# A two-block transformer kernel on one core: the on-chip buffers are laid out in another order, and one operand is packed more tightly

## The reference, cut to what matters

```
h = x
h = layer_norm(a*h + sparse_attention(h));  h = layer_norm(a*h + mlp(h))      # layer A, 16 heads, top-128 keys
h = layer_norm(a*h + gated_linear(h));      h = layer_norm(a*h + mlp(h))      # layer B, 4 heads, chunks of 64
# second block
p    = modulate(rms_norm(h)) @ w_in
mix  = concat[attention(8 heads), bidirectional_mlstm(4 heads)] @ w_out
h    = h + g1 * mix
h    = h + g2 * (silu(u @ w_gate) * (u @ w_up)) @ w_down,   u = modulate(rms_norm(h))
out  = rms_norm(h) * g
```

## Time and profile before

| | |
|---|---|
| time, three runs | 1869.84, 1871.6, 1872.71 us, median 1871.6 us |
| the profiled execution | 1871.6 us, its span from first to last instruction 1869.8 us |
| granted clock of TensorE, mean | 0.997 |
| busy | PE 98%, DVE 61%, ACT 40%, POOL 6% |
| moved by DMA | 189.34 MB, mean 101 GB/s |

### The profile page before, as it was taken

How to read it: one execution, slowest core, us unless ns; L and a number is a source line. 1 busy time by engine, 2 the same in 40 slices (tenths; PEclk the granted TensorE clock), 3 DMA queues, 4 the chain that set the end, 5 groups by cost and what they waited for, 6 DMA issues and landing times.

```text
span 1869.8 us, 22776 instructions
## 1 busy us (share of the span) xinstructions
PE 1825.8 (98%) x9140; PEld 1490.0 (80%) x9140; DVE 1132.9 (61%) x1953; ACT 744.2 (40%) x1177; POOL 117.3 (6%) x117
## 2 busy tenths in 40 slices
PE   9999999999999999999999999999998999999998
PEld 7775788888888888878888888778656898888886
DVE  4987676555557687577654455786766543333338
ACT  4548343222333543645322233365655452222222
POOL 0341000000000063000000000000011000000000
PEclk9999999999999999999999999999999999999999
DMA  6220415434443121141533333222102313223221
GB/s 211 68 74 30 169 46 203 135 135 144 160 146 115 46 86 51 50 154 46 180 113 131 117 113 120 85 90 93 46 24 78 114 45 114 90 91 112 90 91 45
DMA packets 120185, 189.34 MB, mean 101 GB/s; under 512 B 7800, under 2 KB 72536, under 8 KB 117008
## 3 DMA queue, kind: packets, MB, share of 16 engines
q1 hardware_dynamic: 118688, 183.08, 29.5%
q0 software_dynamic: 1392, 4.82, 0.9%
HBM read 185.72 MB, written 2.16 MB: 100 GB/s over the span
## 4 chain that ended last, share of the span: by engine, by line
PE 83%; DVE 10%; ACT 5%; issue 2%; DMA 0%; DVEq 0%; ACTq 0%
PE bank L652 10%; PE bank L654 10%; PE bank L653 10%; PE bank L841 7%; PE bank L843 7%; PE bank L842 7%; PE bank L626 3%; PE bank L628 3%; PE bank L627 3%; PE bank L901 2%; PE bank L876 2%; DVE gb L2306 2%; PE bank L674 2%; PE bank L885 2%; PE bank L676 2%
## 5 line engine op out<-in xcount | busy, mean ns | idle before, releaser
L1945 DVE TENSOR_TENSOR wl<-raw,wh 128x2048 fp32r<-128x2048 f32 (+1 forms) x137 | 308.4, 2256 | 203.1 <-ACT wh L1296 202.7
L1296 ACT ACTIVATE wh<-raw 128x2048 fp32r<-128x2048 f32 (+1 forms) x142 | 265.3, 1882 | 225.5 <-PE bank L843 89.0
L652 PE MATMUL bank<-xh,wh 128*128 128x512 f32 (+1 forms) x872 | 340.1, 390 | 1.1 <-DVE wl L1945 1.1
L654 PE MATMUL bank<-xl,wh 128*128 128x512 f32 (+1 forms) x872 | 339.3, 389 | 0.0
L653 PE MATMUL bank<-xh,wl 128*128 128x512 f32 (+1 forms) x872 | 339.3, 389 | 0.0
L841 PE MATMUL bank<-wh,uh 128*128 128x512 f32 x592 | 230.4, 389 | 0.5 <-DVE wl L1945 0.5
L842 PE MATMUL bank<-wl,uh 128*128 128x512 f32 x592 | 230.3, 389 | 0.0
L843 PE MATMUL bank<-wh,ul 128*128 128x512 f32 x592 | 230.3, 389 | 0.0
L652 PEld LDWEIGHTS bank<-xh,wh 128*128 128x128 f32 (+1 forms) x872 | 163.3, 187 | 37.5 <-DVE wl L1945 1.9
L654 PEld LDWEIGHTS bank<-xl,wh 128*128 128x128 f32 (+1 forms) x872 | 163.3, 187 | 34.5
L653 PEld LDWEIGHTS bank<-xh,wl 128*128 128x128 f32 (+1 forms) x872 | 163.3, 187 | 34.1
(11 more groups left out here) (362 smaller groups left out, 2945.0 us busy)
## 6 DMA issues: line engine op xcount, KB each, us to landing
raw<-in_mlp_w_up SPq DMA_DIRECT2D x32, 1024.0 KB, 6.1
raw<-in_mlp_w_down SPq DMA_DIRECT2D x32, 1024.0 KB, 5.0
raw<-in_w_ada SPq DMA_DIRECT2D x24, 1024.0 KB, 5.0
raw<-in_b_w_in SPq DMA_DIRECT2D x12, 1024.0 KB, 5.2
raw<-in_w_gate SPq DMA_DIRECT2D x11, 1024.0 KB, 5.2
raw<-in_w_up SPq DMA_DIRECT2D x11, 1024.0 KB, 5.1
raw<-in_w_in SPq DMA_DIRECT2D x10, 1024.0 KB, 5.0
raw<-in_w_down SPq DMA_DIRECT2D x10, 1024.0 KB, 4.9
```

Source lines behind the costliest of these rows:

```text
L652: pe.matmul(o, H[:, k, c], xh[:, k, :], start=k == 0, stop=False)
L654: step = pe.matmul(o, H[:, k, c], xl[:, k, :], start=False, stop=k == 7)
L1296: act.activation(slots[slot_of[i]][0][:, 0:n], raw[:, i % NRAW, 0:n], ACT.Copy).then_inc(*s_high.up(i))
L1945: dve.tensor_tensor(L[:, 0:n], raw[:, i % NRAW, 0:n], H[:, 0:n].bitcast(F), ALU.subtract).then_inc(*s_low.up(i))
```

## The change

The declarations are put in another order, `margin` and `end` go, `A` grows from 13312 to 13344 numbers a partition, the rows of `vx` shrink from 144 to 130 numbers (so that the matmul streams whole rows, still 130), and what lay behind `vx` in `A` moves down by 224 numbers. `Mr` gets the 512 numbers that this leaves at the end of `A`, in place of a range within the first 2048 numbers.

```diff
         h = sb("h", [P, T, D])
+        with nc.sbuf_tensor("xf", [P, 8192], F) as xf:
+            pass
+        xh = sb("xh", [P, 8, SEQ], R)
+        xl = sb("xl", [P, 8, SEQ], R)
         raw = sb("raw", [P, NRAW, CH])
+        wh = sb("wh", [P, NHL, CH], R)
+        wl = sb("wl", [P, NHL, CH], R)
...
+        C = sb("C", [P, C_END])
         LM = sb("LM", [P, 8 * P], U8)
-        rot = sb("rot", [P, 2, T, 16])
...
+        gb = sb("gb", [P, 2048])
         small = sb("small", [P, 648])
...
-        sb("margin", [P, 56])
-        gb = sb("gb", [P, 2048])
...
-        with nc.sbuf_tensor("A", [P, 13312], F) as A:
+        with nc.sbuf_tensor("A", [P, 13344], F) as A:
             pass
...
-        sb("end", [P, 1024])
...
-        inv_b = [A[:, 12032:12544], A[:, 12544:13056]]
+        inv_b = [A[:, 11808:12320], A[:, 12320:12832]]
...
-        vx = A[:, 9728:12032].rearrange("p (t h n) -> p t h n", t=T, h=4)
+        vx = A[:, 9728:11808].rearrange("p (t h n) -> p t h n", t=T, h=4)
...
-        kd2 = A[:, 12032:13056].rearrange("p (t n) -> p t n", t=T)
-        Mr = [A[32 * d:32 * d + 4, 1536:2048] for d in range(2)]
+        kd2 = A[:, 11808:12832].rearrange("p (t n) -> p t n", t=T)
+        Mr = [A[32 * d:32 * d + 4, 12832:13344] for d in range(2)]
...
-                            step = pe.matmul(bank[b][:, o:o + 130], STm[m % 2][:, q, t * P:(t + 1) * P], vx[:, q, hh, 0:130],
+                            step = pe.matmul(bank[b][:, o:o + 130], STm[m % 2][:, q, t * P:(t + 1) * P], vx[:, q, hh, :],
```

More of the change, by code:

```diff
@@ L320, in program @@
         h = sb("h", [P, T, D])
-        raw = sb("raw", [P, NRAW, CH])
-        LM = sb("LM", [P, 8 * P], U8)
-        rot = sb("rot", [P, 2, T, 16])
[L324 to L341, removed]
-        sb("margin", [P, 56])
-        gb = sb("gb", [P, 2048])
         with nc.sbuf_tensor("xf", [P, 8192], F) as xf:
@@ L348, in program @@
         xl = sb("xl", [P, 8, SEQ], R)
+        raw = sb("raw", [P, NRAW, CH])
         wh = sb("wh", [P, NHL, CH], R)
@@ L358, in program @@
         ul = sb("ul", [P, 2, 4, SEQ], R)
-        with nc.sbuf_tensor("A", [P, 13312], F) as A:
+        C = sb("C", [P, C_END])
+        LM = sb("LM", [P, 8 * P], U8)
+        gb = sb("gb", [P, 2048])
+        small = sb("small", [P, 648])
+        stats = sb("stats", [P, T, 2, 6])
+        mv = sb("mv", [P, T, 2])
+        rsv = sb("rsv", [P, 64])
+        rsy = sb("rsy", [P, 64])
+        rsa = sb("rsa", [P, 64])
+        rsh = sb("rsh", [P, 64])
+        posi = sb("posi", [P, T], I32)
+        rot = sb("rot", [P, 2, T, 16])
+        iw = sb("iw", [P, T, 8])
+        m8 = sb("m8", [P, 8])
+        att = sb("att", [P, 3, 16, T])
+        ssq = sb("ssq", [P, T, 4])
+        ebl = sb("ebl", [P, 4, 4])
+        s32 = sb("s32", [P, 16])
+        root = sb("root", [P, 16])
+        epsilon = sb("epsilon", [P, 2])
+        q_rms = sb("q_rms", [P, 32])
+        gg = sb("gg", [P, T, 16])
+        g2_ = sb("g2_", [P, T, 16])
+        acol = sb("acol", [P, 2, T, 4])
+        ecol = sb("ecol", [P, 2, T, 4])
+        den = sb("den", [P, 2, 2, 2])
+        with nc.sbuf_tensor("A", [P, 13344], F) as A:
             pass
```

## The result

| | before | after |
|---|---|---|
| median of 5 runs | 1871.6 us (1869.84 to 1874.81) | 1883.14 us (1882.68 to 1883.57) |
| ratio, 95% interval | | 1.0062, 1.005 to 1.0074 |
| profiled execution, its span | 1871.6, 1869.8 us | 1881.6, 1879.8 us |
| mean granted clock | 0.997 | 0.998 |

The forecast was 1871.6 us with a range of 1868 to 1877. The measured time lies beyond it on the slow side.

What follows compares the result with a forecast made beforehand. PE was taken to bound the kernel, as a sum over some 9140 matmuls in fixed order. Every part of the change came to 0 us, so the 1869.8 us span plus 1.8 around it gave 1871.6 us, range 1868 to 1877.

Steps and rivals of the forecast that it cites:

- What bounds the kernel: Whole kernel: PE, 98% busy, runs some 9140 matmuls in fixed order; 512 columns take 0.2257 us, 12.4 ns not columns.
- The instruction streams: All five engines: same operations, shapes and waits in the same order, so nothing may start earlier; 0 us.
- `vx`: Rows at 520 bytes, streamed by 160 matmuls of L1203: starts 8 past a multiple of 16 cost 0 us.
- DVE and ACT: Buffers 32 past a multiple of 64: convolution starts at nearly any multiple of 4 cost at most 8 ns; 0 us.
- POOL: L2885 and L2903 at the new starts: taken as 0 us, with ends of -0.9 and +0.9.
- DMA: Transfers to `gb`, `A` and `C` at new offsets: 0 to 0.4 us, taken as 0; 0.04 us for each spread.
- Weight loads: PE loads from buffers 32 past a multiple of 64: hidden beside the matmul before unless 38 ns longer; 0 us.
- Moving operands of PE: 1,552 matmuls streaming from `A`, `gb`, slots 2 and 3: taken as 0; upper end a second 12.4 ns each, 19.2 us.
- rival A: Those 1,552 PE matmuls slow down when streaming from 32 past 64: 1881.2 us at half, 1890.8 at whole; chance 0.11.
- Buffers now 128 past a multiple of 256, and other distances between buffers: `xh` to `pl` and `C`: starts at any multiple of 64, and where another buffer lies, cost PE nothing; 0 us.
- Rival B: mLSTM stage: PE's pause and clock drop near 1412 us go or grow; if gone, 1866.3 us, chance 0.05.
- C: Rope and gate jobs start earlier as `Mr` shares no queries' bytes; held impossible, 1871.6 us; chance 0.74 with the forecast.
- D: DMA pays for the starts: 0.4 us on the chain, 1 us in the mLSTM stage, 1873.0 us; within a shared 0.08.

Runs made afterwards that it cites:

- e4c_A_same_mod256: The kernel after with `A` moved on by 96 bytes: 1871.47 us against 1871.72 for the kernel before, ratio 1.0002.
- e3_before_all_plus32: The kernel before with everything from `xh` to `A` moved on by 32 bytes: 1872.58 us against 1873.20, ratio 0.9999.
- e2_before_A_plus32: The kernel before with only `A` moved on by 32 bytes: 1882.78 us, ratio 1.0054.
- m2c_differences: TensorE alone, no kernel: 48 split matmuls per operand pair, buffers 2048 bytes apart, differences in 16-byte steps; 226.7 ns a matmul at difference 0.
- m1_starts: TensorE alone, no kernel: 48 matmuls per streamed and loaded pair, buffers 8320 bytes apart; 226.7 ns a matmul where both start alike.

## Why the prediction was wrong

*What bounds the kernel* held: the time is a sum over PE's matmuls, and the 10 us came as longer matmuls, in no wait. One reading in it is a little off: by the starts of before, a matmul of 512 columns takes 226.7 ns and not 225.7, as the count of the earlier trace rows takes in a few narrow ones and one at the edge, so 13.3 ns and not 12.4 are not columns. Nothing hangs on it. By its own parts the chances add up to 0.83 for the same time and 0.11 for slower, not 0.82 and 0.12.

*The instruction streams, `vx`, DVE and ACT, POOL, DMA* held at 0. L2628 takes 751 ns (752 before), L2882 858 (866), and `e4c_A_same_mod256` bounds all of them and the plain matmuls together at -0.07 to +0.12%, that is -1.3 to +2.2 us. The Trainium skill's rule on DMA alignment ("DMA: Bandwidth & Descriptors", How a descriptor splits into AXI transactions), estimated at 0.04 us a spread, stays unseen within that; the page speaks of bytes that are fetched, and `A` is the side that is written in these spreads.

*Weight loads* is the step that failed. It said: "A usual load takes 188 ns of a 226 ns step and lies beside the matmul before; it would have to grow by 38 ns before PE saw it. 0 us." The load did not grow, 187 to 188 ns after as before, and yet the step went from 226.7 to 233.2 ns on the 1,340 matmuls that load from slots 2 and 3: 8.7 us, three quarters of the loss. A load's recorded duration doesn't show what its start does to the matmul that runs with it, so neither that duration nor the room beside it bounds anything.

A sign stood in the trace of before, in the very stretch of the earlier trace rows. The step looked there at the loads (141 ns, odd and even rows alike) and not at the matmuls beside them. The timeline of PE in that chunk, kernel before:

```profile
35.68 0.39 PE L652 MATMUL bank<-xh,wh 128*72 128x512 f32 x1
...
38.46 0.40 PE L652 MATMUL bank<-xh,wh 128*72 128x512 f32 x1
```

Twelve steps in 2.78 us: 0.2317 us each (0.2310 by the exact starts), not the 0.2267 of the chunk shown above. So the old kernel already had matmuls that were 4 to 5 ns dearer beside loads that looked free; times the 1,340 that is some 6 us. It is a sign and not the rule: here the loads are 72 columns wide and start at multiples of 288 bytes, and the three steps with difference 0 take 235 ns each, those with 96 only 227 to 229. What the narrower load changes was not tested.

*Moving operands of PE* was mis-sized: taken as 0 in a range of 0 to 19.2 us, measured +3.2 us. Of the 528 split ones counted, the 480 of 512 columns pay 6.7 ns each, and of the 1,024 plain ones none. But most plain ones had nothing to show: L876, L1024 and L1189 have both operands in `A`, so their difference did not change. Half of the second 12.4 ns was the size that rival A had named for each. The value was taken from "the nearest rows", the 272-wide chunk, and that is where the argument broke: those matmuls do start at every multiple of 64, but 272 columns don't pay even in the kernel after (the 48 whose difference changed take 0.4 ns less). Rows of another width were no near rows.

*Buffers now 128 past a multiple of 256, and other distances between buffers* came to 0, but only because of what stayed equal: `xh`, `wh` and `uh` had moved together (+0.3 ns on 4,486 matmuls, and 0.0 ns in `e4c_A_same_mod256`). The sentence that one pace in the earlier trace rows shows no effect of where another operand lies was empty: in the old layout all buffers of the split matmuls began at 0 modulo 256, so nothing there could have shown it.

*Rival A* (a moving operand 32 past a multiple of 64 costs PE something, chance 0.11) was nearest: the right engine, the right sign, and its half size, 1881.2 us, within 2 us of the time. Its rule is wrong. The lines it named first, L1024, L876 and L1203, did not slow down (277, 640 and 287 ns after; 276, 640 and 294 before); L674, which it named too, did, by 0.6 us; the largest part came from loads, which it left out; and `e3_before_all_plus32` puts every moving operand there at no price.

*Rival B* (the pause and its clock) did happen, faster by some 2 us in one execution, and explains none of the medians. *C* held as a part: `Mr` frees nothing. *D* is not seen: PE's first matmul starts at 2.66 us in both, and the identity's DMA takes 1.87 us against 1.88.

What stays open is why the chip does it. The price hangs on two operands of PE, what is streamed and what is loaded. Whether the load that counts is a matmul's own or its successor's, the few mixed steps don't settle, and both seem to bear on it: in the kernel after, 11 matmuls with an own difference of 0, whose successor's weights lie at 96 against what they stream, went from 226.6 to 236.7 ns, and 13 the other way round from 226.6 to 229.3; in `e2_before_A_plus32` the latter went to 232.5. Nor do these runs show why differences of 240 bytes (and 124) are free and 16 is not. Whether wide plain matmuls would pay is open as well: of some 220 steps of 384 and 512 columns only 24 had their difference changed (no change in pace), and the other plain ones with a changed difference, which pay nothing, have at most 256 columns.

## What to carry to other kernels

When a layout is changed, work out for each hot matmul of this kind (split, 512 columns) the start of the streamed operand minus that of the loaded one modulo 256, before and after, and keep it at 0; a pad of 96 bytes took this loss back whole. When a price is bounded by "the nearest rows", ask whether the quantity could have varied in them at all, and read the pace of the matmuls from their starts, not the duration of the instruction that seems to be affected. A loss of 0.6% that is spread as 3% over 1,800 equal steps is visible in one timeline of twenty rows.

## What the runs showed of the hardware

- A split matmul of 512 columns with a load of 128 columns takes 226.7 ns when both operands start alike modulo 256 bytes, and 229 to 240 ns at nearly all other differences; 240 and 124 are the exceptions (226.7). The absolute start hardly matters at difference 0: both moved by 32, 64 or 128 bytes, 226.7 to 227.4 ns in `m2c_differences`, and no loss in `e3_before_all_plus32` (ratio 0.9999). At differences of 80 and 112, with starts off a multiple of 32, it does, by 1.2 and 2.3 ns.
- It needs no other engine: `m1_starts` and `m2c_differences` show it with the rest of the core idle. The Trainium skill ("SBUF — State Buffer", SBUF: two separate sides) says that within the engine side only the port pair of GpSimd and VectorE causes contention and that PE never waits on anyone. The runs agree as far as other engines go (226.7 ns beside busy DVE and ACT in the MLPs, and 226.7 alone); the price between PE's own two operands, up to 8 ns on 226.7 at differences in steps of 16 bytes and 13 ns at 132, it does not foresee.
- The price depends on width and kind. At 256 columns equal starts are the slowest (120.0 ns, 116.7 to 119.7 elsewhere). At 384 a difference of 96 costs 3.3 ns, 128 costs 2.6 and 192 costs 1.4, and 32 or 64 none. At 128 columns (111.7 ns), and at 272 in the kernel after, there is none. The plain matmuls of up to 256 columns whose difference changed show none either; wide ones were hardly tested.
- The load's recorded duration stays at 187 to 188 ns at either pace.
